# Joints around four blocks of seven-product pairs rearranged, and their middle tiles taken in parts of 8 and 14

## The reference: what is computed

```python
def _swiglu(h, w_gate_up, w_down):
    g, u = jnp.split(h @ w_gate_up, 2, axis=-1)
    return (jax.nn.silu(g) * u) @ w_down
...
        x = x + FFN_RES_WEIGHT * _swiglu(_rmsnorm(x, ffn1_norm[layer]), ...)
        x = x + _hybrid_mixer(...)
        x = x + FFN_RES_WEIGHT * _swiglu(_rmsnorm(x, ffn2_norm[layer]), ...)
```

## Time and profile before

| what | value |
|---|---|
| median of 3 runs | 3530.12 us (3528.09 to 3537.2) |
| the profiled execution, its time | 3532.91 us |
| its span, from first to last instruction | 3531.1 us |
| mean granted TensorE clock | 0.976 |
| busy: PE, DVE, ACT, POOL | 3348.2, 1901.6, 1470.9, 1630.4 us |

### The profile page before, as it was taken

One profiled execution on the slowest core, in us unless ns is written; L12 is line 12 of the kernel. 1 busy time (PEld: TensorE's weight loads), 2 busy tenths in 40 slices (PEclk: granted clock), 3 DMA queues, 4 the chain that ended last, 5 costly groups with the idle time before them and its releaser, 6 DMA issues.

```text
span 3531.1 us, 47177 instructions
## 1 busy us (share of the span) xinstructions
PE 3348.2 (95%) x18766; PEld 2828.2 (80%) x18766; DVE 1901.6 (54%) x3348; ACT 1470.9 (42%) x2582; POOL 1630.4 (46%) x952
## 2 busy tenths in 40 slices
PE   8999999999999889999998999899999988999998
PEld 5767788877778779797776989799887768989776
DVE  3266766622331468173565836674553767636655
ACT  4533324523222355154455524453343655424543
POOL 3313455563344347464524645455445335645332
PEclk9999999999999989999999999999999999999999
DMA  7212233432343323233312232223233112323221
GB/s 272 68 48 66 97 99 127 160 122 85 135 136 116 128 76 105 87 108 107 90 33 73 99 107 94 80 100 106 88 111 106 44 57 91 110 87 107 73 66 54
DMA packets 102217, 345.95 MB, mean 98 GB/s; under 512 B 12173, under 2 KB 12557, under 8 KB 101838
## 3 DMA queue, kind: packets, MB, share of 16 engines
q1 hardware_dynamic: 101200, 341.10, 30.1%
q10 hardware_dynamic: 798, 1.85, 0.1%
HBM read 336.08 MB, written 2.10 MB: 96 GB/s over the span
## 4 chain that ended last, share of the span: by engine, by line
PE 80%; DVE 9%; ACT 5%; DMA 3%; POOL 2%; issue 1%; SPq 0%; DVEq 0%; ACTq 0%
PE ps L1398 14%; PE ps L1399 13%; PE ps L1400 13%; PE ps L1433 8%; PE ps L1435 8%; PE ps L1434 8%; PE ps L1458 2%; PE ps L1459 2%; PE ps L1460 2%; PE ps L1730 2%; DVE t L2451 1%; DMA t<-in_w_ffi 1%; PE ps L1757 1%; POOL t L3079 1%; DMA t<-in_w_ada 1%
## 5 line engine op out<-in xcount | busy, mean ns | idle before, releaser
L3079 POOL TENSOR_TENSOR t<-t,t 128x1024 fp32r<-128x1024 f32 (+2 forms) x408 | 921.7, 2265 | 1336.0 <-ACT t L1817 1323.5
L1398 PE MATMUL ps<-t,t 128*128 128x512 f32 x2608 | 1052.9, 404 | 71.6 <-POOL t L3079 61.1
L1399 PE MATMUL ps<-t,t 128*128 128x512 f32 x2608 | 1028.1, 394 | 0.0
L1400 PE MATMUL ps<-t,t 128*128 128x512 f32 x2608 | 1026.1, 393 | 0.0
L3089 POOL TENSOR_TENSOR t<-t,t 128x512 fp32r<-128x512 f32 x440 | 569.7, 1321 | 430.7 <-ACT t L1832 430.3
L1433 PE MATMUL ps<-t,t 128*128 128x256 f32 x2464 | 707.7, 287 | 47.7 <-DVE t L2327 15.3
L1434 PE MATMUL ps<-t,t 128*128 128x256 f32 x2464 | 702.4, 285 | 0.0
L1435 PE MATMUL ps<-t,t 128*128 128x256 f32 x2464 | 701.9, 285 | 0.0
L1398 PEld LDWEIGHTS ps<-t,t 128*128 128x128 f32 x2608 | 495.9, 190 | 208.2 <-issue 50.3
L1817 ACT CAST t<-t 128x1024 fp32r<-128x1024 f32 (+2 forms) x412 | 400.7, 975 | 541.8 <-PE ps L1400 304.0
L1400 PEld LDWEIGHTS ps<-t,t 128*128 128x128 f32 x2608 | 495.2, 190 | 110.1
(11 more groups left out here) (331 smaller groups left out, 3750.4 us busy)
## 6 DMA issues: line engine op xcount, KB each, us to landing
t<-in_w_f1i SPq DMA_DIRECT2D x88, 512.0 KB, 3.8
t<-in_w_f2i SPq DMA_DIRECT2D x88, 512.0 KB, 3.7
t<-in_w_ada SPq DMA_DIRECT2D x72, 512.0 KB, 3.7
t<-in_w_ffi SPq DMA_DIRECT2D x44, 512.0 KB, 5.4
t<-in_w_f1o SPq DMA_DIRECT2D x32, 512.0 KB, 4.0
t<-in_w_f2o SPq DMA_DIRECT2D x32, 512.0 KB, 4.1
t<-in_w_gate SPq DMA_DIRECT2D x24, 512.0 KB, 4.1
t<-in_w_out SPq DMA_DIRECT2D x48, 256.0 KB, 2.6
```

The costliest lines, as they stand in the source:

```text
L1398: e.matmul(out, wh[:, at], X.hi[c][:, 0:N], start=c == first, stop=False)
L1399: e.matmul(out, wh[:, at], X.lo[c][:, 0:N], start=False, stop=False)
L1400: m = e.matmul(out, wl[:, at], X.hi[c][:, 0:N], start=False, stop=c == final)
L3079: e.tensor_tensor(k.WL[k.slot[n]][:, 0:w], k.raw[:, j % NRAW, 0:w], f(k.WH[k.slot[n]][:, 0:w]), ALU.subtract).then_inc(*k.rest.inc(('rest' ...
```

## The change

It has six parts. `PAIRS` gives the four blocks of pairs 8 and then 14 middle tiles; `ff1` keeps 14 and 8. `ffn` puts each T of a down projection ahead of `begin_pair`. `m.side` is stepped once for each plain tile, and twice beside each output tile of the first down projection. The tiles of the first network's output (`final_tile`) are made beside e of `f1_0`, no longer within the pairs. `renew` staggers what stands behind an output tile ahead of pairs: the lows of one output tile stand behind the residual of the next, and the weights of the first pair begin two output tiles earlier than the last. `first_products` is an order of its own for pair 0, in which p6 and p7 are done for three of four activation tiles before the fourth; banks A, C and Q are held for it. Last, the squares have three buffers where they had four, so that the copy of p1 needs not wait for the sum of squares.

```diff
-PARTS = ((0, 14), (14, 8))
+PARTS, PAIRS = (((0, 14), (14, 8)), ((0, 8), (8, 14)))
...
-    for part, (first, count) in enumerate(PARTS):
+    for part, (first, count) in enumerate(PARTS if m.scale is None else PAIRS):
         (plain if m.scale is None else fours)(on, m, first, count)
         after = (m.next, 0) if part else (None if m.scale is None else m, first + count)
         for n in range(KT):
-            if after[0] is not None:
+            on.T(('ed'[part], m.tag, n), m.wo, n, m.mid, kt=count, first=first)
+            for _ in range(n < 4 if part else 2):
+                next(m.side, None)
+            key = ('ed'[part], m.tag, n)
+            if part == 0:
+                if m.whole is not None:
+                    on.final_tile(m.whole, n, 'final_g')
                 begin_pair(on, *after, n)
-            on.T(('ed'[part], m.tag, n), m.wo, n, m.mid, kt=count, first=first)
-            if part:
-                on.residual(m.res, n, ('d', m.tag, n), ('filled', ('u', m.tag, FF - 1)))
+                on.partial(m.res, n, key)
+            elif m.res.four:
+                renew(on, m.res, n, key, ('filled', ('u', m.tag, FF - 1)), *after)
             else:
-                on.partial(m.res, n, ('e', m.tag, n))
+                on.residual(m.res, n, key, ('filled', ('u', m.tag, FF - 1)))
...
+def renew(on, res, n, key, since, m, i):
+
+    on.residual(res, n, key, since)
+    if 0 < n < 7:
+        on.sum_lows(res, n - 1)
+    on.sum_parts(res, n)
+    if n < 6:
+        on.squares(res, n)
+        on.add_squares(res, n)
+    on.sum_highs(res, n)
+    if n == 5:
+        on.sums(m, i, 'S1')
+        on.round(m, i, 'A11')
+        on.round(m, i, 'S1')
+        on.minus(m, i, 'A11')
+        on.minus(m, i, 'S1')
+    if n == 6:
+        on.sums(m, i, 'S2')
+        on.sum_lows(res, n)
+        on.round(m, i, 'S2')
+        on.minus(m, i, 'S2')
+        on.sums(m, i, 'S3')
+        on.round(m, i, 'S3')
+        on.minus(m, i, 'S3')
+        on.squares(res, n)
+    if n == 7:
+        on.sum_lows(res, n)
+        on.add_squares(res, 6)
+        on.squares(res, n)
+        on.add_squares(res, n)
...
-        for _ in range(2 if i > 2 else 0):
+        if i > 2:
             next(m.side, None)
+
+
+def first_products(on, m):
+
+    for j in m.before.later:
+        on.last_lows(m.before, j)
+    for js in ((0, 1, 2), (3,)):
+        on.product(m, 0, 'p6', js)
+        on.product(m, 0, 'p7', js)
+    on.second_sum(m, 0)
+    on.third_sum(m, 0)
+    on.minus(m, 1, 'S1')
+    on.product(m, 0, 'p4')
+    on.up_sum(m, 0)
...
     for n in range(KT):
-        begin_pair(on, m, 0, n)
         on.T(('out2_' + L, n), 'out' + L, n, at.OA, kt=4)
-        on.residual(res, n, ('out2_' + L, n), ('filled', ('fqk', L, 7)))
+        renew(on, res, n, ('out2_' + L, n), ('filled', ('fqk', L, 7)), m, 0)
```

More of the change, by code:

```diff
@@ L150 @@
 class Sum:
-    last = 7
+    last, end = (7, 4)
     bank = False
@@ L160, in slots, with short @@
             return square_ring(k)
-        return ring(k, 'sq ' + self.tag, k.tmp[self.first:], self.since)
+        return ring(k, 'sq ' + self.tag, k.tmp[self.first:self.end], self.since)
+def short(sq):
+    sq.end = 3
+    return sq
 def banked(sq):
@@ L691, in begin_pair @@
         on.round(m, i, 'S2')
-    if n == KT - 1:
+    if m is not None and n == KT - 1:
         on.sums(m, i, 'S3')
@@ L708, in plain @@
         on.ffn_up(m, i)
-        for _ in range(2 if i > 2 else 0):
+        if i > 2:
             next(m.side, None)
+def first_products(on, m):
[9 more added lines that the diff above has]
+    on.up_sum(m, 0)
+    on.sums(m, 1, 'S2')
+    on.round(m, 1, 'S2')
+    on.roots(m.scale, 4 if m.whole else 2)
+    on.product(m, 0, 'p2')
+    on.sums(m, 1, 'S3')
+    on.round(m, 1, 'S3')
+    on.round(m, 1, 'A22')
+    on.minus(m, 1, 'S2')
+    on.minus(m, 1, 'S3')
+    on.minus(m, 1, 'A22')
+    on.round(m, 1, 'A12')
+    on.minus(m, 1, 'A12')
+    on.product(m, 0, 'p3')
+    on.row(m.scale)
+    on.sums(m, 1, 'S4')
+    on.round(m, 1, 'S4')
+    on.minus(m, 1, 'S4')
 def fours(on, m, first, count):
@@ L748, in fours @@
             on.round(m, i + 1, 'S2')
[L749 to L756, removed]
+        on.product(m, i, 'p6')
         if not begin:
@@ L1421, in product @@
         opens = p in ('p1', 'p5', 'p6', 'p7')
-        out = (self.take(k.banks, *key, hold=i == 0 and bank == 'A') if opens and js[0] == 0 else self.bank(*key))[:, col:col + 256]
+        out = (self.take(k.banks, *key, hold=i == 0 and bank in 'AC') if opens and js[0] == 0 else self.bank(*key))[:, col:col + 256]
         if i == 1 and p == 'p6':
             k.banks.let(('A', m.tag, 0))
+            k.banks.let(('C', m.tag, 0))
         self.wait_ge('rest', m.tag, i, piece)
@@ L2802, in residual @@
         self.square(res.sum, n, x, ('x', res.tag, n))
-        if res.four:
-            self.sum_lows(res.A, n)
-            if n % 2 and n // 2 not in res.later:
-                self.last_lows(res, n // 2)
     def partial(self, res, n, key):
@@ L3141, in residual, with add_squares @@
     def residual(self, res, n, key, since=None):
+        if not res.four:
+            self.add_squares(res, n)
+    def add_squares(self, res, n):
         self.square(res.sum, n, self.k.X[:, n, :], ('x', res.tag, n))
```

106 lines of the change are left out of this document (67 added, 39 removed).

## The result

The changed kernel takes 3420.55 us, the median of 4 runs (3420.31 to 3421.45), beside 3529.22 us for the kernel before: a ratio of 0.9688, 95% interval 0.9671 to 0.9705. The forecast was 3419 us.

A forecast was written before the change was run, and what follows sets the result against it. TensorE, busy 3348 of 3531.1 us, was taken as the bound, with only time between its busy stretches to win. 30.1 + 26.6 + 54.5 = 111.2 us off 3532.9 gives 3421.7, the median 2.8 lower: 3419 us, range 3390 to 3455.

The forecast's parts named there:

- ff1: Plain tiles of `ff1`: with one read of `side` each, weight units load in time; 30.1 us won, bounds 16 and 32.
- SP's 169.4 us of waits: In `ff1`: the weight-load queue's waits for DVE's reads of `side`, taken to say what the remaining 32.1 us were.
- the second rival: Beside e: reads hold up the ring as in the tiles, 3.7 us for 7 output tiles, 26 us; 3445 us, chance 0.10.
- Middle joints: Four joints, one in each block: TensorE's wait of 4.14 us and the half clock behind it go, 26.6 us won.
- Joints ahead of pairs: Four joints ahead of pairs: 88 us lost there, 33.6 estimated to stay, 54.5 won; bounds 15 and 80 us.
- The last output tile's chain: Joints ahead of pairs: chain of some 3.6 us beside 33 matmuls or 3.9 us; 0.2 us stays at each.
- The wait for A22's rest: Joints ahead of pairs: p4 needs A22 after 7.6 us, TensorE is through p7 after 5.7; 2.0 us stays at each.
- The stretch of half clock: Joints ahead of pairs: one stretch as at a middle joint, 2.5 us staying at each.
- DVE beside POOL: Joints ahead of pairs: four last lows took 4.00 us where 2.8 are enough; 2.0 us stays at each for all such.
- The backlog of out2: The two out2 joints only: sums and rests of S1, S2 and S3 between residuals, five times 0.69, 3.4 us staying.
- the first rival: Joints ahead of pairs: DVE stays the bound, some eight instructions each wait 1 us for POOL; 3451 us, chance 0.17.
- Bank order: Pairs: held banks assumed to cost nothing; the fourth rival had the pairs' rhythm break, 3595 us at 2 us a pair, chance 0.03.

The follow-up runs named there:

- the run that has the whole gain: The kernel before with one step of `side` for a plain tile and two beside each output tile of the first down projection: 3500.05 us, ratio 0.9912.

## Why the prediction was right

By its steps:

- **`ff1`, 30.1 us forecast, 32.1 measured** (31.9 alone). The late rests are gone, as forecast; the 2 us that I kept back for a late unit don't exist in the tiles. My sign for the mechanism, SP's 169.4 us of waits, was misread: it is 160.6 us in the run that has the whole gain. The reads beside e cost a little, not nothing: e is 3.2 us longer than before from its first to its last `partial` (1014.18 to 1084.71 us after), of which 1.84 are a close of a group that moved there out of the tiles and 1.15 a wait for a rest. That wait is the second rival's mechanism; it came once, where the rival had 26 us of it.
- **Middle joints, 26.6 forecast, 26.2 measured.** The size was right, the reason half so. I named two causes for the freed ACT, that all units are rounded ahead of A11 and that places fall free earlier. The second isn't needed: with 14 and 8 tiles the place of S2 falls free as late as ever, and only the first counts.
- **Joints ahead of pairs, 54.5 forecast, 54.9 measured**, with each joint within 1.2 us. This is partly luck, since the items of what stays were mis-sized both ways. The last output tile's chain, 0.2 us each: 1.04 ahead of `f1_0`, none ahead of `f1_1`. My own working gave no wait at all, a chain of 3.6 us beside matmuls of 3.9, and the new order puts three quarters of p7 there too. The wait for A22's rest, 2.0 us each: 0.65, 2.16, none and 3.48. The stretch of half clock, 2.5 us each: none at the two joints behind d, 1.2 and 3.1 at the others. DVE beside POOL, 2.0 us: four lows took 6.82 us of DVE's time where 2.8 were enough, but TensorE waited only 0.56 us for them ahead of `f2_0`. The backlog of out2, 3.4: waits of 0.50 and 1.55. Not in my list at all: `up_sum` of the first and second pair (1.47 and 1.37 us) and the reciprocal (1.34).
- **A cause that I didn't name.** I put the 88 us at these joints down to DVE's pace beside the output tiles. But 15.3 of the 59.5 us of idle time were the wait of the second pair for the first middle tile's rest, 3.8 us in each block. It went with the place of the norm's row and the first gate in the new order of pair 0. The forecast had this time in it only because it counted all that was lost and took off what stays.
- **Independent items.** The step that didn't hold is that I added these items up as if each could be removed by itself. The run with A22 early shows that they stand behind one another: 5.7 us of waits taken away gave 0.1 us at the marks and 1.2 between medians of different chips.
- **DVE against POOL, the first rival.** Its mechanism is there, and its price of 8 us a joint isn't. In the changed kernel, a DVE instruction with an input in PSUM takes the same time wherever it stands, within 10% for each line and shape. One with all inputs in SBUF takes up to 2.7 times its least time in the lines shown here (length in ns: least, median, most):

```profile
L2448 DVE TENSOR_TENSOR t<-t,ps x176: 635/679/690, 1218.9 to 3073.9; 128x512 f32<-128x512 f32 x176
...
L2435 DVE TENSOR_TENSOR ps<-t x88: 687/1430/1824, 1211.9 to 3066.5; 128x512 f32<-128x512 f32 x88
...
L2875 DVE SCALAR_TENSOR_TENSOR t<-t,t,t x16: 741/1751/1777, 1193.4 to 2823.2; 128x512 fp32r<-128x512 f32 x16
```

By the Trainium skill ("SBUF — State Buffer", section "SBUF: two separate sides"), a DVE instruction with two inputs in SBUF and a GpSimd one that reads SBUF take turns, each for its whole length. The trace agrees as to which instructions suffer. Only the price is less than a full turn: low and rest alternate every 1.70 us where 0.74 and 1.30 alone would be 2.04.

- **The pairs and the first tile of e**: the pairs are as long as before (the marks of pairs 2 to 7 of `f2_0` show 65.4 to 65.6 us won throughout; the largest loss from one pair to the next is 0.3 us), and no new wait of e appears in the blocks of pairs. Bank order and the shorter part cost nothing, as assumed.

## What to carry to other kernels

Ask of a stalled engine what is queued behind it, not how long it stands: ACT's wait of 3.01 us cost 4.1 us or nothing, by two lines' order. When two edits cure one wait, one of them is free to be undone; only runs of each alone tell. And a list of waits at a joint is no list of gains: take one away, and read who comes next before the second is priced.

## What the runs showed of the hardware

The clock behind a wait isn't fixed by the kernel. In the attention of the first layer TensorE waits 1.74 us for ACT, in the changed kernel and in its repeated run alike. Behind that wait the granted clock fell to a mean between the levels of 1.2 and 2.4 GHz in the first execution, and stayed at full speed in the second (length, busy time, granted clock, DMA):

```profile
1758.00:1762.00 4.00, 4.00 (x16) 0.69 0.02 4
...
1756.00:1760.00 4.00, 4.00 (x33) 1.00 0.00 0
```

Over this stretch the two executions come 1.6 us apart. The joint ahead of `f2_0` shows the same, with a twist: in stretches of 50 us the mean clock was 0.97 in the one execution and 0.90 in the other, and yet the joint won 12.0 and 11.9 us. TensorE was idle for 9.1 us where the clock was high and for 6.7 where it was low.

Ahead of the mixer of each layer TensorE waits 3.05 us for a rest, in every kernel here. In the kernel before, the granted clock stayed at 1.00 behind it both times. In the changed kernel it fell both times, in the repeated run too:

```profile
1600.00:1604.00 4.00, 4.00 (x11) 0.57 0.49 131
```

That costs 0.4 of 4 us, 1.7. Over the other kernels it goes either way: with 14 and 8 tiles it stayed at 1.00 at both places. So the clock moves marks by 1 to 3 us between executions, the two executions of the changed kernel differ by up to 3.0 us at a mark, and no gain of that size should be read from one profile. What decides it I can't tell; it wasn't tried.
